# The last shift-mix of an even round moved ahead of the chunk states in VectorE's order, in a hybrid decoder trunk

## What is computed

```python
def step(state, inp):                     # HGRN2, chunk by chunk
    ...
    o = attn @ vc + (qc * exp(G)) @ state # "bhts,bhsv" and "bhtk,bhkv"
    state = exp(g_last) * state + (kc * exp(g_last - G)).T @ vc
    return state, o

zb = zb + (_shift(zb) - zb) * mu          # RWKV-7: r, k and v are mixed with the token before
rb, kb, vb, wlr, alr = jnp.split(zb, ...)
```

## Time and profile before

| | |
|---|---|
| median of 3 runs | 1300.94 us (1300.34 to 1301.23) |
| the profiled execution | 1301.23 us |
| its span in the trace | 1299.4 us |
| TensorE busy | 1210.2 us, 93% |
| TensorE's mean granted clock | 0.978 of full speed |
| VectorE, ScalarE, GpSimd busy | 58%, 34%, 47% |

### The profile page before, as it was taken

How to read it: one execution, slowest core, us unless ns; L and a number is a source line. 1 busy time by engine, 2 the same in 40 slices (tenths; PEclk the granted TensorE clock), 3 DMA queues, 4 the chain that set the end, 5 groups by cost and what they waited for, 6 DMA issues and landing times.

```text
span 1299.4 us, 30234 instructions
## 1 busy us (share of the span) xinstructions
PE 1210.2 (93%) x11354; PEld 994.5 (77%) x11354; DVE 757.3 (58%) x1343; ACT 441.2 (34%) x835; POOL 616.9 (47%) x584
## 2 busy tenths in 40 slices
PE   2899999999999999999997989998699999989995
PEld 1788879888888798888885868877477777768873
DVE  6655474474564744745646331267646866867447
ACT  4342242242422422424324331132425243443123
POOL 3643451443424514424242137778366574648771
PEclk9999999999999999999998979999799999999997
DMA  5221120221211202212112023433122222322331
GB/s 207 77 64 42 49 68 26 66 60 34 60 42 53 65 26 66 60 34 59 42 54 61 18 99 97 113 91 96 49 81 81 66 89 65 89 57 75 96 89 65
DMA packets 46723, 88.66 MB, mean 68 GB/s; under 512 B 5808, under 2 KB 6832, under 8 KB 46384
## 3 DMA queue, kind: packets, MB, share of 16 engines
q1 hardware_dynamic: 44352, 82.70, 21.8%
q10 hardware_dynamic: 2288, 4.72, 1.1%
HBM read 85.30 MB, written 2.10 MB: 67 GB/s over the span
## 4 chain that ended last, share of the span: by engine, by line
PE 80%; DVE 13%; issue 3%; ACT 3%; DMA 0%; SPq 0%; DVEq 0%; ACTq 0%
PE psum L320 78%; DVE mix L1344 3%; ACT mix L931 2%; DVE mix L1368 2%; PE psum L868 1%; DVE mix L1872 1%; DVE mix L1790 1%; DVE h_split L1348 1%; DVE mix L1801 1%; DVE mix L1864 1%; DVE mix L1855 1%; PE psum L440 1%; DVE mix L1870 1%; DVE y L1876 1%; DMA mix<-xT 0%
## 5 line engine op out<-in xcount | busy, mean ns | idle before, releaser
L320 PE MATMUL psum<-h_split,w_hi 128*128 128x512 f32 x2320 | 751.1, 405 | 29.6 <-DVE mix L1445 11.1
L320 PEld LDWEIGHTS psum<-h_split,w_hi 128*128 128x128 f32 x2320 | 429.6, 191 | 137.8 <-issue 42.2
L303 POOL TENSOR_SCALAR w_hi<-w_raw 128x512 fp32r<-128x512 f32 x290 | 207.1, 714 | 632.4 <-PE psum L320 498.5
L320 PE MATMUL psum<-h_split,w_lo 128*128 128x512 f32 x1160 | 457.8, 395 | 0.0
L305 POOL TENSOR_TENSOR w_lo<-w_raw,w_hi 128x512 fp32r<-128x512 f32 x290 | 410.3, 1415 | 24.2
L320 PE MATMUL psum<-mix 64*64 64x64 f32 (+5 forms) x7552 | 340.7, 239 | 11.0 <-ACT mix L931 4.3
L320 PEld LDWEIGHTS psum<-mix 64*64 64x64 f32 (+3 forms) x7552 | 310.1, 142 | 53.3 <-issue 34.6
L931 ACT ACTIVATE mix<-psum 128x512 f32<-128x512 f32 (+4 forms) x292 | 136.9, 489 | 460.7 <-PE psum L320 326.6
L320 PEld LDWEIGHTS psum<-h_split,w_lo 128*128 128x128 f32 x1160 | 220.7, 190 | 48.3
L931 ACT ACTIVATE mix<-mix 128x512 f32<-128x512 f32 (+2 forms) x274 | 142.0, 551 | 173.5 <-DVE mix L1773 73.5
L1438 DVE COPY_PREDICATED mix<-mask,psum 128x128 f32<-128x128 uint8 (+2 forms) x272 | 108.8, 440 | 106.7 <-PE psum L320 93.7
(11 more groups left out here) (113 smaller groups left out, 623.0 us busy)
## 6 DMA issues: line engine op xcount, KB each, us to landing
w_raw<-wall SPq DMA_DIRECT2D x290, 256.0 KB, 2.6
mix<-xT SPq DMA_DIRECT2D x4, 512.0 KB, 5.1
mix<-mask_f SPq DMA_DIRECT2D x1, 2048.0 KB, 11.5
mix<-xT ACTq DMA_DIRECT2D x1, 2048.0 KB, 7.8
out<-mix SPq DMA_DIRECT2D x8, 256.0 KB, 2.1
mix<-pT ACTq DMA_DIRECT2D x2, 512.0 KB, 3.7
mix<-lru_w ACTq DMA_DIRECT2D x4, 256.0 KB, 3.4
mix<-w2a ACTq DMA_DIRECT2D x16, 32.0 KB, 2.3
```

What stands on the lines that cost most here:

```text
L303: pool.tensor_scalar(w_hi[:, slot, :, :], w_raw[:, slot, :], 1.0, 0.0, ALU.mult, ALU.add).then_inc(sem["w_hi"], 1)
L320: return pe.matmul(o, lhsT, rhs, start=start, stop=stop, skip_group_check=True)
```

## The change

In VectorE's program the last two steps of `even_round` with `head=True` change places:

```diff
                     masked(i, 5)
                     masked(i, 6)
                     masked(i, 7)
+                    mixed(i, 2, 7, wv)
                     states(i)
-                    mixed(i, 2, 7, wv)
```

## The result

| | before | after |
|---|---|---|
| median | 1301.09 us (6 runs, 1300.34 to 1302.39) | 1311.62 us (6 runs, 1308.51 to 1313.85) |
| ratio | | 1.0078 (95% interval 1.0061 to 1.0094) |
| profiled execution, span | 1301.23, 1299.4 us | 1311.31, 1309.5 us |

The account below looks back on a forecast made before the run. TensorE, busy 93% of the span, was taken to bound the kernel. Two calls at 1.40 us and six at 1.48 add 11.7 to 1301.23, giving 1312.9; less 0.29 to the median, 1312.6 us, range 1310.0 to 1316.5.

Parts of the forecast that it names:

- The mix gains nothing: VectorE, end of a call: `mixed` still waits for ScalarE's copy, starts at 691.77 us as before; idle 3.7 us, not 1.13.
- The states' new start and length: VectorE behind the mix: the copy starts 0.67 us after it, at 692.44; third state ready at 693.50 us, not 690.64.
- The hole: TensorE in `hg_outputs`, waiting for the states at each call's end: 1.40 us in two calls, 1.48 in six.
- The delay is kept: After `hg_outputs`: every engine starts the next call 1.48 us later, and TensorE has no waits to catch up with.
- GpSimd's hold: Rival: moved `states` overlaps GpSimd's split and is held up 0.4 us a call, 3.2 in all; 1315.8 us, chance 0.10.
- The clock: Rival: the hole drops TensorE's clock to half in each call, 8 x 5 = 40 us; 1353 us, chance 0.04.
- Absorption and relief: Rivals: later TensorE waits absorb the delay (1301, partly 1304 to 1309; 0.06); an earlier mix saves 8.5 us (1292.4; 0.02).

Follow-up runs that it names:

- the last state alone: Against the kernel before: copy and second state stay ahead of the mix, only the third state moves behind it; 1306.92 us, ratio 1.0050.
- the longer hold: Changed kernel plus an unneeded VectorE copy of 384 columns ahead of `states`; 1318.45 us, again 1316.89 us (ratios 1.0144, 1.0124 to the kernel before).
- `low_rank` first: On TensorE, next call's `low_rank` ahead of `hg_outputs`: with the changed VectorE order 1307.48 us, again 1311.30; with the order of the kernel before 1301.36.

## Why the prediction was right, point by point

- *The mix gains nothing.* Shown: it starts 1.00 us after the first record of `hg_outputs`, as before, and waits 3.69 us where 3.7 was said.
- *The states' new start and length.* The copy starts 0.66 us after the mix's start (702.10 to 702.76; said 0.67), and the last is ready 1.71 us after the mix's start (703.08 + 0.73 - 702.10; said 1.73).
- *The hole.* Said 1.40 us twice and 1.48 six times; measured 1.46 and 1.53, each 0.05 to 0.06 more. The sum is 12.1 and not 11.7 us. The term that was a little too small is the restart of TensorE. The last product's two records took 0.49 us where I took 0.45. It started 1.43 us later than before (said 1.45) and ended 1.53 later (said 1.51), and `low_rank` behind it was late by the 1.53 of its end, not by a value in between. I had named waits for L1344 as well, of 1.0 to 1.5 us together with those for L1496; the profile shows only the wait for L1496, 0.87 us twice and 0.95 six times, and the rest as products that start further apart (0.38 us and not 0.22).
- *The delay is kept.* Shown by the ruler (30.12 us in both kernels behind the readers' step), by the last state alone (6.4 us by the trace, 6.5 measured) and by the longer hold (16.7 by the trace and 18.7 measured the first time, 16.2 and 16.1 the second).
- *GpSimd's hold.* Refuted. The split ran from 702.15 to 703.41 us, beside the copy and the first of the two other steps. The copy took 0.28 us and the two others 0.73, no more than alone. The copy of 17 columns at L1642, now behind the split, took 0.17 us in place of 0.69, which fits that the split had held it up.
- *The clock.* It did not fall in any of 40 holes of the changed kernel, whose wait is 0.87 to 0.95 us. With waits of 1.34 to 1.42 us it fell in one of eight, twice.
- *Absorption and relief.* Neither; the idle time ahead of the mix only grew. In the five profiles of the changed kernel all that lies behind the last scan took 601.8 to 604.3 us, against 605.0 in the one of the kernel before; with one profile of that kernel I can't say whether the difference belongs to the change.

The forecast of 1312.6 us lies 1.0 us above the median of one set of runs and 0.2 above that of the other; in the microseconds of the ratios, 11.7 said and 10.1 and 11.8 measured. A hit this close has some luck in it: what the forecast lacked is the spread of about 2 us either way by which executions of this kernel differ. The traces put it into the start, the stage of the block inverses and all that lies behind the even layer; for `low_rank` first a cause was seen, for the kernels before and after it stays open.

## What to carry to other kernels

VectorE served its queue in order: with the changed order the copy came 0.66 us behind the start of the mix, though its own input had long been there. So a step that waits for a late input should stand behind the steps that others wait for. What decides is when each input comes (here 689.58 against 691.77 us) and who is idle meanwhile. Price such a swap by the consumer that sets the pace: the time from its last work that needs nothing to the new time of its input; the idle time of the swapped engine says nothing. And before moving work on the engine that sets the pace to fill a hole, look what hangs on its results on the other engines: here that chain had less room than the 2.0 us by which the outputs moved.

## What was not expected of the hardware

Two instructions of VectorE and GpSimd that read SBUF side by side can make a program bistable: with starts 0.00 to 0.03 us apart, the same stretch took 1.71 or 2.83 us on VectorE, call by call (one call of seven and four of seven in two profiles), and one kernel's medians were 1307.5 and 1311.3 us in two sets of runs. And the clock's answer to a hole is not a matter of the hole alone: of sixteen like ones of 1.34 to 1.42 us, each amid dense work, two brought it down, one of them among the shorter.
